# Three shared PSUM banks for the products of an FFN pair, added up by TensorE

## The reference, cut to what matters

```python
def _swiglu(h, wg, wu, wd):
    return (jax.nn.silu(h @ wg) * (h @ wu)) @ wd

def _layer(x, mod, p, tables, ctx_ckv, ctx_krope):
    ...
    h = _rmsnorm(x, p["norm_ffn1"]) * (1 + sc1) + sh1
    x = x + 0.5 * g1 * _swiglu(h, p["w_ffn1_gate"], p["w_ffn1_up"], p["w_ffn1_down"])
    ...
    h = _rmsnorm(x, p["norm_ffn2"]) * (1 + sc3) + sh3
    x = x + 0.5 * g3 * _swiglu(h, p["w_ffn2_gate"], p["w_ffn2_up"], p["w_ffn2_down"])
```

## Time and profile before

| | us |
|---|---|
| median of 3 runs | 2764.28 |
| runs, lowest to highest | 2762.7 to 2765.19 |
| span of the profiled execution | 2759.8 |
| TensorE busy | 2689.4 (97%) |
| VectorE busy | 2017.3 (73%) |
| ScalarE busy | 1216.1 (44%) |
| GpSimd busy | 622.6 (23%) |

### The profile page before, as it was taken

How to read it: one execution, slowest core, us unless ns; L and a number is a source line. 1 busy time by engine, 2 the same in 40 slices (tenths; PEclk the granted TensorE clock), 3 DMA queues, 4 the chain that set the end, 5 groups by cost and what they waited for, 6 DMA issues and landing times. The chain is left out here.

```text
span 2759.8 us, 44748 instructions
## 1 busy us (share of the span) xinstructions
PE 2689.4 (97%) x17878; PEld 2536.0 (92%) x17878; DVE 2017.3 (73%) x2736; ACT 1216.1 (44%) x1998; POOL 622.6 (23%) x323
## 2 busy tenths in 40 slices
PE   6999999999999999999999999999999999999997
PEld 3999999977799999999989999999778999999997
DVE  6878878766534788887888879787664358776876
ACT  5533435556422543343564335355563236443433
POOL 1322422022100124232321413210220002242230
PEclk9999999999999999999999999999999999999999
DMA  6445432210121253423224444322101222212312
GB/s 239 152 147 161 146 123 68 72 56 26 43 84 63 92 168 116 130 99 109 93 101 152 139 159 145 102 75 67 46 27 64 74 65 85 92 63 84 105 49 77
DMA packets 86446, 273.02 MB, mean 99 GB/s; under 512 B 8736, under 2 KB 10016, under 8 KB 86112
## 3 DMA queue, kind: packets, MB, share of 16 engines
q1 hardware_dynamic: 84800, 265.60, 29.1%
q10 hardware_dynamic: 1440, 4.56, 0.5%
HBM read 267.21 MB, written 2.92 MB: 98 GB/s over the span
## 5 line engine op out<-in xcount | busy, mean ns | idle before, releaser
L624 POOL TENSOR_TENSOR sums_raw<-raw_pairs 128x1024 f32<-128x1024 f32 x88 | 238.3, 2708 | 1627.9 <-DVE weights_lo L1706 1050.2
L652 PE MATMUL ps<-h_hi,weights_hi 128*128 128x322 f32 (+1 forms) x1408 | 440.3, 313 | 8.6 <-DVE t_lo L1706 3.1
L656 PE MATMUL ps<-h_hi,weights_lo 128*128 128x322 f32 (+1 forms) x1408 | 437.4, 311 | 0.0
L654 PE MATMUL ps<-h_lo,weights_hi 128*128 128x322 f32 (+1 forms) x1408 | 436.8, 310 | 0.0
L1706 DVE TENSOR_TENSOR weights_lo<-sums_raw,weights_hi 128x1024 fp32r<-128x1024 f32 (+2 forms) x296 | 329.7, 1114 | 56.5 <-ACT weights_hi L1237 26.7
L652 PE MATMUL ps<-t_hi,weights_hi 128*128 128x322 f32 (+1 forms) x1056 | 332.2, 315 | 5.3 <-DVE h_lo L1706 5.3
L652 PE MATMUL ps<-a_hi,weights_hi 128*128 128x320 f32 x1408 | 325.1, 312 | 3.3 <-DVE tmp L1884 2.5
L656 PE MATMUL ps<-t_hi,weights_lo 128*128 128x322 f32 (+1 forms) x1056 | 327.5, 310 | 0.0
L654 PE MATMUL ps<-t_lo,weights_hi 128*128 128x322 f32 (+1 forms) x1056 | 326.4, 309 | 0.0
L654 PE MATMUL ps<-a_lo,weights_hi 128*128 128x320 f32 x1408 | 321.5, 309 | 0.0
L656 PE MATMUL ps<-a_hi,weights_lo 128*128 128x320 f32 x1408 | 321.5, 309 | 0.0
(11 more groups left out here) (273 smaller groups left out, 5680.6 us busy)
## 6 DMA issues: line engine op xcount, KB each, us to landing
raw_pairs<-in_w_up SPq DMA_DIRECT2D x87, 1024.0 KB, 4.9
wm<-in_w_mod SPq DMA_DIRECT2D x88, 512.0 KB, 3.9
raw<-in_w_merge SPq DMA_DIRECT2D x32, 704.0 KB, 4.0
sums_raw<-in_w_down SPq DMA_DIRECT2D x56, 384.0 KB, 3.2
wm<-in_w_mod SPq DMA_DIRECT2D x80, 256.0 KB, 3.0
sums_raw<-in_w_down SPq DMA_DIRECT2D x64, 320.0 KB, 3.0
raw<-in_w_in SPq DMA_DIRECT2D x16, 512.0 KB, 3.6
raw<-in_w_out SPq DMA_DIRECT2D x16, 512.0 KB, 3.5
```

The source lines that it names most:

```text
L624: nc.gpsimd.tensor_tensor(sums_raw[:, UNIT:3 * UNIT].rearrange("p (s c) -> p s c", s=2), w.rearrange("p (s c) -> p s c", s=2)[:, :, 0:UNIT ...
L652: nc.tensor.matmul(out, whi, v, start=first, stop=False)
L654: nc.tensor.matmul(out, whi, v, start=False, stop=False)
L656: mm = nc.tensor.matmul(out, wlo, v, start=False, stop=last)
```

## The change

I call a chunk's first pair *lone* (the code's word) and the other 72 of the 88 pairs *joint*. Lone pairs are computed as before, in other banks. In a joint pair TensorE adds products up by itself, by going on with a sum in the same bank (a first matmul that doesn't clear it), in three banks of which neighbouring pairs use two sets in turn:

- bank A: P1, then P2 on top. Ahead of P2, ScalarE copies P1 into bank C.
- bank C: the copy of P1, then P6 on top (U2), which ScalarE copies to SBUF (`copy_u2`); then P7 on top (U3), which ScalarE copies to SBUF (`copy_u3`); then P4 on top.
- bank B: P5, which `c22` reads and adds to the copy of U3; then P3 on top, which `c12` reads and adds to the copy of U2.

VectorE's `u2`, `u2_p5` and `u3` are gone in joint pairs. `c11` and `c21` multiply the finished bank by the norm on their way out of PSUM, and `gate_scaled` and `up_scaled` have the first 320 columns left. On VectorE `c22` and `up_scaled` now stand ahead of `lo_s(g+1)`. The down tiles begin with the first double bank in place of the second, and D0 waits for `c11` of the last pair only. The diff, cut:

```diff
-NAMES = {n: of for of, n in DONE.items()}
-UP_BANKS = 6
+FIRST_BANKS = {"P1": 0, "P2": 5, "P3": 3, "P4": 4, "P5": 2, "P6": 4, "P7": 0}
+
+
+def lone(pair):
+
+    return chunk_of(pair)[1]
+
+
+def lone_count(pair):
+    return pair // PAIRS * 4 + chunk_of(pair)[0] + 1
+
+
+def joint_count(pair):
+    return pair + 1 - lone_count(pair)
 
 
 def up_bank(pair, name):
 
-    f, t = divmod(pair, PAIRS)
-    first = f * PAIRS + FIRSTS[f][chunk_of(pair)[0]]
-    return (DONE[pair, name] - DONE[first, "P1"]) % UP_BANKS
+    if lone(pair):
+        return FIRST_BANKS[name]
+    f = pair // PAIRS
+    other = (pair % PAIRS - FIRSTS[f][chunk_of(pair)[0]]) % 2
+    return {"P1": 0, "P2": 0, "P5": 2, "P3": 2, "P6": 4, "P7": 4, "P4": 4}[name] + other
...
             def up_product(g, name, cols, weights, xhi, xlo, before=None):
 
-                b, n = up_bank(g, name), DONE[g, name]
-                first = g - g % PAIRS + FIRSTS[g // PAIRS][chunk_of(g)[0]]
-                if n - DONE[first, "P1"] >= UP_BANKS:
-                    held, which = NAMES[n - UP_BANKS]
-                    pe.wait_ge({"P1": s_a1, "P2": s_c11, "P6": s_u2, "P5": s_c22, "P7": s_u3, "P4": s_c21,
-                                "P3": s_c12}[which], held + 1)
+                b, onto = up_bank(g, name), not lone(g) and name not in ("P1", "P5")
...
-                    mm = product([bank(b, 0, cols)], whi, wlo, [xhi[i]], [xlo[i]], i == 0, i == KT // 2 - 1)
+                    mm = product([bank(b, 0, cols)], whi, wlo, [xhi[i]], [xlo[i]], i == 0, i == KT // 2 - 1, onto)
...
                     def p3():
                         pe.wait_ge(s_lo34, g + 1)
+                        if not lone(g):
+                            pe.wait_ge(s_c22, g + 1)
                         up_product(g, "P3", HALF, unit(5), first_half(h_hi, 1), first_half(h_lo, 1))
 
                     if start:
...
                         pe.wait_ge(s_lo12, g + 1)
+                        if not lone(g):
+                            pe.wait_ge(s_a1, g + 1)
                         up_product(g, "P2", ext, unit(1), second_half(h_hi, 1), second_half(h_lo, 1))
...
+                    if not lone(g):
+                        if lone(g - 1):
+                            pe.wait_ge(s_c12, g)
+                        elif lone(g - 2):
+                            pe.wait_ge(s_c22, g - 1)
+                        else:
+                            pe.wait_ge(s_c12, g - 1)
                     up_product(g, "P5", HALF, unit(3), differences(t_hi, 0, HALF), differences(t_lo, 0, HALF))
...
                     pe.wait_ge(s_lo34, g + 1)
+                    if lone(g):
+                        pe.wait_ge(s_a1, g + 1)
+                    else:
+                        pe.wait_ge(s_u2c, joint_count(g))
                     up_product(g, "P7", HALF, unit(6), first_half(h_hi, 0), first_half(h_lo, 0))
...
                     pe.wait_ge(s_lo22, g + 1)
+                    if lone(g):
+                        pe.wait_ge(s_usum, lone_count(g) * 3 - 2)
+                    else:
+                        pe.wait_ge(s_u3c, joint_count(g))
                     up_product(g, "P4", ext, unit(2), differences(t_hi, TB, TW), differences(t_lo, TB, TW))
...
-                        out = halves(pair((j + 1) % 3))
+                        out = halves(pair(j % 3))
...
                             if j == 0:
-                                pe.wait_ge(s_c22, last + 1)
-                                pe.wait_ge(s_c21, last + 1)
+                                pe.wait_ge(s_c11, last + 1)
...
             def copy_a1(g):
                 act.wait_ge(s_product, DONE[g, "P1"])
-                act.wait_ge(s_u2, g)
-                act.wait_ge(s_tlo, (g // PAIRS + 1) * KT // 2)
-                nc.scalar.activation(p1_copy, bank(up_bank(g, "P1"), 0, TB - HALF), ACT.Copy).then_inc(s_a1, 1)
+                if lone(g):
+                    act.wait_ge(s_c21, g)
+                    act.wait_ge(s_tlo, (g // PAIRS + 1) * KT // 2)
+                    to = p1_copy
+                else:
+                    if lone(g - 1):
+                        act.wait_ge(s_c11, g)
+                    else:
+                        act.wait_ge(s_c21, g - 1)
+                    to = bank(up_bank(g, "P6"), 0, TB - HALF)
+                nc.scalar.activation(to, bank(up_bank(g, "P1"), 0, TB - HALF), ACT.Copy).then_inc(s_a1, 1)
+
+            def copy_u2(g):
+                act.wait_ge(s_product, DONE[g, "P6"])
+                act.wait_ge(s_c12, g)
+                nc.scalar.activation(u2_copy, bank(up_bank(g, "P6"), 0, HALF), ACT.Copy).then_inc(s_u2c, 1)
+
+            def copy_u3(g):
+                act.wait_ge(s_product, DONE[g, "P7"])
+                act.wait_ge(s_c22, g)
+                nc.scalar.activation(u3_copy, bank(up_bank(g, "P7"), 0, HALF), ACT.Copy).then_inc(s_u3c, 1)
...
                 act.wait_ge(s_usc, g + 1)
+                act.wait_ge(s_c21, g + 1)
...
                     if not first:
+                        copy_u2(g)
                         a_part(g - 1)
                     if last:
                         hi_down(step, c, 0)
+                        copy_u3(g)
                     elif g == g0:
                         diagonal(step)
                         hi_s(g + 1)
...
                         rows_copy(step)
                     else:
                         hi_s(g + 1)
+                        if not first:
+                            copy_u3(g)
                         copy_a1(g + 1)
...
             def c11(g):
                 dve.wait_ge(s_product, DONE[g, "P2"])
-                dve.wait_ge(s_a1, g + 1)
                 dve.wait_ge(s_prod, g)
-                tt(ga[:, HALF:TB], bank(up_bank(g, "P2"), 0, TB - HALF), p1_copy, ALU.add).then_inc(s_c11, 1)
+                if lone(g):
+                    dve.wait_ge(s_a1, g + 1)
+                    ins = tt(ga[:, HALF:TB], bank(up_bank(g, "P2"), 0, TB - HALF), p1_copy, ALU.add)
+                else:
+                    ins = tt(ga[:, HALF:TB], bank(up_bank(g, "P2"), 0, TB - HALF), r_one[:, HALF:TB], ALU.mult)
+                ins.then_inc(s_c11, 1)
...
             def c22(g):
-                dve.wait_ge(s_u3, g + 1)
                 dve.wait_ge(s_alo, g + START)
-                tt(ub[:, 0:HALF], bank(up_bank(g, "P5"), 0, HALF), u_sum[:, 0:HALF], ALU.add).then_inc(s_c22, 1)
+                if lone(g):
+                    dve.wait_ge(s_usum, lone_count(g) * 3)
+                    whole = u_sum[:, 0:HALF]
+                else:
+                    dve.wait_ge(s_u3c, joint_count(g))
+                    whole = u3_copy
+                tt(ub[:, 0:HALF], bank(up_bank(g, "P5"), 0, HALF), whole, ALU.add).then_inc(s_c22, 1)
...
             def gate_scaled(g):
                 dve.wait_ge(s_c11, g + 1)
                 dve.wait_ge(s_c12, g + 1)
-                tt(ga, ga, r_one[:], ALU.mult).then_inc(s_gsc, 1)
+                if lone(g):
+                    tt(ga, ga, r_one[:], ALU.mult).then_inc(s_gsc, 1)
+                else:
+                    tt(ga[:, 0:HALF], ga[:, 0:HALF], rstd[:, 0:HALF], ALU.mult).then_inc(s_gsc, 1)
...
                     c11(g)
-                    u2(g)
+                    if first:
+                        u2(g)
                     if following:
                         lo_12(g + 1)
-                    u2_p5(g)
+                    if first:
+                        u2_p5(g)
                     if g == g0:
                         c12(g)
                         inverse_columns(nn, step)
-                    if not first:
+                    if first:
+                        u3(g)
+                        c22(g)
+                    else:
                         a_rest(g - 1)
-                    u3(g)
-                    c22(g)
+                        c22(g)
+                        up_scaled(g)
                     if last:
                         lo_down(step, c, 0)
                     else:
                         lo_s(g + 1)
                     c21(g)
-                    up_scaled(g)
+                    if first:
+                        up_scaled(g)
...
-                        update(ORDER[k], pair((k + 1) % 3), half_g, 0)
+                        update(ORDER[k], pair(k % 3), half_g, 0)
```

51 lines of the change are left out of this document (35 added, 16 removed).

## The result

| | before | changed |
|---|---|---|
| median, us | 2764.74 (4 runs, 2762.7 to 2765.62) | 2800.39 (4 runs, 2795.36 to 2802.22) |
| ratio, 95% interval | 1 | 1.0129 [1.0115, 1.0144] |
| span of the profiled execution | 2759.8 | 2800.4 |

The changed kernel is 35.6 us slower by the medians. The forecast was 2793, 28.5 us slower, with a range of 2774 to 2812.

A forecast was written before the change was run, and what follows sets the result against it. The prediction took TensorE, busy 97% of the span, to bound the kernel. New waits of 36.0 us less 7.5 us of gains gave +28.5 us, so 2793 us, with a range of 2774 to 2812.

The forecast's parts named there:

- about 100 us or more: Sign of a right forecast: VectorE's busy time falls by about this much, with no gain in the span.
- The chain in the 22 pairs: Joint pairs behind a joint pair, without modulation work: P4 waits for `copy_u3`, 0.33 late and 0.10 more; 9.5 us.
- The mis-sized term: Wherever TensorE waits for a ScalarE copy: TensorE follows 0.05 us after ScalarE ends, the second matmul 0.10 late.
- Last pairs: 16 last pairs: P4 follows P7 at once, so the copy of U3 costs 0.77 us each; 11.9 us in all.
- Pairs with cover: Pairs with modulation matmuls between P1 and P4: no cost; four with only a small transpose there: 1.1 us.
- the second pairs of an FFN: P7 waits for `copy_u2`, late because ScalarE changes its table for the SiLU: 3 x 0.93 = 2.8 us.
- P3 costs nothing: P3 waits for `c22`, whose 0.49 us on VectorE fits within P4's 1.77 us: no cost.
- The gains: Waits that go at D0, D1, P7 and for low parts, with a clock fall and a late matmul: 7.5 us.
- TensorE waits at last pairs alone: Rival: P4 never waits in joint pairs going on to another; 2768 us, not slower; chance 0.13, half of it faster.
- GpSimd faster: Rival: fewer VectorE adds make GpSimd's sums 0.41 us earlier; 2779 us; chance 0.07.
- The relief does not reach the sums: Rival: `lo_34` stays where it was, so the 22 joint pairs wait longer at P4; 2808 us; chance 0.14.
- The clock falls with the waits: Rival: some 25 new TensorE waits each bring a clock fall of 1.4 us; 2828 us; chance 0.06.

The follow-up runs named there:

- Experiment 1: The changed kernel with `copy_u3` ahead of `hi_s` on ScalarE in joint pairs that are not last: 2776.97 us, ratio to before 1.0046.
- experiment 2: The changed kernel with `copy_u3` ahead of the first `hi_down` in last pairs: 2796.24 us, ratio to before 1.0115.
- experiment 4: The changed kernel with the copy of U3 made twice, the first into a scratch tile nobody reads: 2819.05 us, ratio to before 1.0193.
- experiment 6: The changed kernel with `gated` on VectorE waiting for `copy_u2` in pairs not last of a chunk: 2800.33 us, ratio to before 1.013.
- experiment 5: The changed kernel with `c22` and `up_scaled` behind `lo_s` again on VectorE in joint pairs not last: 2803.89 us, ratio to before 1.0145.
- experiment 7: Changed kernel, `copy_u3` ahead of `hi_s`, last pairs' copies and products reordered: 2764.09 us; also with early SiLU table load: 2757.99. Control, kernel before with that load alone: 2762.72.

## Why the prediction came out as it did

**What bounds the kernel: right.** TensorE does. VectorE's 88.6 us bought nothing but the few waits TensorE had for it, and each new wait on TensorE was paid in full. The sign of "about 100 us or more" was missed, and the trace shows where: VectorE's low parts are longer in the changed kernel, those of the product (`a_rest`) sum to 134.3 us over 88 pairs, where it was 111.5, and those of the loaded weights to 291.0, where it was 266.7 (those of the sums are 9.3 shorter). In pair 30 the first two run beside GpSimd's sums, as `lo_12` above with 2.29 does.

**The chain in the 22 pairs: right, and close.** `lo_34` at 3.03 after P2 (3.04), `hi_s` at 7.75 (7.76), copy at 8.72 (8.72). P4 came at 9.28, not 9.19. Experiment 1 shows that the queue order is the whole cause in these pairs.

**The mis-sized term is the signal from a copy to TensorE.** I took 0.05 us from the earlier trace rows. Behind `copy_u3` it is 0.14 (1122.78 to 1122.92), in pair 5 of experiment 2 also 0.14 (127.78 to 127.92). With the second matmul 0.08 late in place of 0.10, a joint pair costs 0.41 + 0.08, not 0.33 + 0.10, and one behind a lone pair 1.04 + 0.08, not 0.95 + 0.10. Pair 67 was put right (2.0 + 0.2, 2.3 forecast); pair 68, behind it, waits 0.95, which I had as one of the 22. Together 1.9 over. The row I took was of another instruction, a scaling of SBUF data for L692. The trace of before has the other value too, and the prediction passed it by: TensorE waits 14 times for an exponential that ScalarE takes of a bank (L1606), and starts 0.14 behind its end each time (here 599.23 to 599.37).

```profile
598.63 0.60 ACT L1606 ACTIVATE tmp<-ps 128x512 f32<-128x512 f32 x1 [0.31 <-PE ps L656]
...
599.37 0.67 PE L1107 MATMUL ps<-tmp,v 128*128 128x512 f32 x1
```

That ScalarE reads PSUM does not decide it, since behind the copy L1181, also out of a bank, it is 0.05. What decides it no run here tells. The second matmul behind the waits for `weights_lo` that I had read is 0.10 late, behind `copy_u3` 0.08.

**Last pairs: 14.8 against 11.9.** A usual one is 0.78 late at P4, not 0.67, by the same signal, and 0.06 more behind it, not 0.10. Pairs 5 and 16 are 0.98 late. That makes 1.2 of the 2.9. The other 1.7 is pair 10, 2.31 late where the other two with a small transpose in that place are 0.64 and 0.65, and where I had written that "the cover of `hi_down` in last pairs is thin". There the load of the down weights was late:

```profile
242.03 0.74 ACT L1271 ACTIVATE weights_hi<-sums_raw 128x640 fp32r<-128x640 f32 x1 [3.51 <-DMA sums_raw<-in_w_down]
242.67 0.42 ACT L1368 ACTIVATE tmp<-ps 128x320 f32<-128x320 f32 x1
...
243.24 0.38 PE L668 MATMUL ps<-t_hi,weights_hi 128*128 128x322 f32 x1 [2.06 <-ACT tmp L1368]
```

`copy_u3` needs no load, but stands behind `hi_down`, which waits for one. In the kernel before, P4 did not depend on that load. The traces of experiments 4 and 6 show the late load too (`hi_down` idle for it 3.23 and 3.04 us), those of 1 and 5 do not (1.53 and 1.31), and their last pairs sum to 12.5 and 12.3 from P7 to P4. It is not pair 10 alone: P4 of pair 54 is 2.65 and 1.55 late in experiments 4 and 6, where it is 0.64 in the changed kernel, and P4 of pair 37 is 1.36 late in experiment 1. With the copy ahead (experiment 2) P4 no longer depends on it.

**Pairs with cover, and the second pairs of an FFN: right** (1.1 and 2.8 forecast, 1.1 + 0.2 and 2.8 found).

**P3 costs nothing: right for the changed kernel,** with less to spare than I wrote; in the order of experiment 5 it is paid for.

**The gains: 7.5 forecast, 9.1 in the trace, but not all of it is real.** The wait of 2.2 us at D0 of pair 43 is gone, as said. The 1.4 us for the slow clock behind it is doubtful. The first window is the kernel before, the second the control kernel of experiment 7, both over the 8.85 us behind that same wait:

```profile
1357.15:1366.00 8.85, 8.85 (x50) 8.85 (x51) 5.97 (x11) 3.51 (x6) 0.00 (x0) 0.81 0.45 135
```

```profile
1361.05:1369.90 8.85, 8.85 (x60) 8.85 (x61) 5.97 (x11) 3.51 (x6) 0.00 (x0) 1.00 0.46 135
```

50 matmuls against 60, after a wait of the same length. A clock that falls in one execution isn't a term of the sum; it is scatter. That this term came out in the table is luck, of which executions were profiled, and the 1.5 us of pair 10 on the other side are so too. The middle of the forecast was 7.1 us too low by the medians, inside the range; the range's own reasons (the second matmuls' 0.10, the gains half as large) were not what moved it.

**The rivals.** *TensorE waits at last pairs alone* falls: P4 waited in the joint pairs, as forecast. *GpSimd faster* falls: the median of L640 is 2816 ns after against 2818 before, with three adds a pair less beside it. What held it was `gated`: with `gated` later it is 2396 (experiment 6). The Trainium skill's rule on two SBUF inputs, which I had weighed against this rival, was right, and this case bears it out. *The relief does not reach the sums* falls with `lo_34` at 3.03. *The clock falls with the waits* falls for the waits of 0.4 to 1.4 us, by experiment 4. Behind waits of 2 us it fell in some traces, and not in others. Behind the wait in pair 10 the window below shows a mean of 0.67; from 244 to 247 us it is 0.50, the lower of the two levels (1.2 GHz).

```profile
243.24:248.39 5.15, 5.15 (x24) 5.15 (x25) 3.14 (x7) 1.65 (x3) 0.00 (x0) 0.67 0.24 64
```

That fall is the 1.5 us of the table's row on pair 10; it too varies from execution to execution. The Trainium skill's account of a clock that swings under frequent short idle spells (TensorE: Matmul & The Clock Gate, section "A second HAM failure mode: psum-queue depth-cycling") is not borne out here for some 50 spells of 0.4 to 1.4 us.

**What stays open.** Why the mixers run a mean clock of 1.00 in one execution and 0.99 in others, and why the load in pair 10 is late in some. Neither was tried. What sets the 0.05 or 0.14 us of a signal is open too, and so is the rest of the difference by place, 2.2 us between the trace's 33.4 without its last row and the medians' 35.6.

## What to carry to other kernels

When a copy is put between two products that share a bank, its place in its engine's queue decides what it costs: ask for each one what stands ahead of it and whether that waits for a third engine, and put it where its engine is idle anyway. Moving work off an engine that nobody waits for gains only the waits there are, and a chain of copies on another engine can cost more than that: here 36 us, all of it got back by moving the copies and changing the order of the products in last pairs. Before an engine's instruction is put off to clear another's way (experiment 6), follow what waits for it, over the other engines too. Where one execution's clock or load was slow, look at a second trace before you count it as a gain.

## What the runs showed of the hardware that I had not expected

- From the end of ScalarE's copy out of PSUM to the first matmul that waits for it: 0.14 us, as behind the 14 waits for L1606 before, where L1251 and L1181 showed 0.05. VectorE started 0.10 after the same copy (1122.78 to 1122.88).
- In three cases a VectorE instruction with two SBUF inputs that started beside a GpSimd add ended its own length less 0.13 or 0.14 us after that add's end: `lo_12` 0.56 (its length alone is 0.69), `gated` 0.69 (0.82), `lo_s` in experiment 5 1.08 (1.22). The other way round, with `gated` 0.26 ahead of it, GpSimd's sum takes 0.42 longer (2.82 against 2.40).
- The granted clock fell behind idle spells of about 2 us in some executions (0.81, 0.67 and 0.67 in the windows above, means over stretches at both levels) and stayed at 1.00 behind the same spell in others.
